# Neighbourhood attention: the keys held as four contiguous column tiles, where one map was read in strided runs

## The reference

```python
def neighbourhood_attention(q, k, v, rpb):        # 8 heads of 64, a grid 64 columns wide
    ...
    c0 = np.clip(cols - WIN_COLS // 2, 0, GRID_W - WIN_COLS)      # window: 8 rows x 16 columns
    ...
        s = jnp.einsum('bqhd,brqchd->bhqrc', q_r, k_win).astype(jnp.float32)
        s = s + bias.transpose(0, 2, 1, 3)[None]
        p = jax.nn.softmax(s.reshape(bsz, H, GRID_W, wr * WIN_COLS), axis=-1)
        return jnp.einsum('bhqrc,brqchd->bqhd', p, v_win)
```

## Time and profile before

| what | value |
|---|---|
| three runs | 3501.95, 3507.84 (median), 3510.64 us |
| the profiled execution | 3500.29 us, its span 3498.5 us |
| mean granted TensorE clock | 0.966 of full speed |
| PE busy | 3202.0 us, 92% |
| DVE busy | 2169.9 us, 62% |
| ACT busy | 1415.3 us, 40% |
| POOL busy | 544.7 us, 16% |

### The profile page before, as it was taken

The page is one execution under the profiler, slowest core; times in us unless marked ns, Lnnn a source line. Parts: engine busy times, 40 slices in busy tenths (PEclk is TensorE's granted clock), DMA queues, the critical chain, the costliest instruction groups (busy, mean ns, idle before and its releaser), DMA issues. The chain is left out here.

```text
span 3498.5 us, 49075 instructions
## 1 busy us (share of the span) xinstructions
PE 3202.0 (92%) x16456; PEld 2663.8 (76%) x16456; DVE 2169.9 (62%) x3352; ACT 1415.3 (40%) x2628; POOL 544.7 (16%) x540
## 2 busy tenths in 40 slices
PE   8999999977999589979939999899998998999999
PEld 6787878765777479967728888678887997888887
DVE  3434536465666589955537666676676997455555
ACT  3343434345766345522223333333333444434443
POOL 2101011012333157735520000000000000000000
PEclk9999999998999899989969999999999999999999
DMA  5354545465331222278852222432233344667776
GB/s 185 127 190 149 193 149 179 136 192 108 85 83 37 68 80 70 65 243 295 275 197 90 102 108 105 144 120 101 97 113 124 134 138 163 215 231 271 244 263 213
DMA packets 394109, 531.94 MB, mean 152 GB/s; under 512 B 126544, under 2 KB 238464, under 8 KB 385328
## 3 DMA queue, kind: packets, MB, share of 16 engines
q1 hardware_dynamic: 378240, 481.97, 42.3%
q0 software_dynamic: 12864, 43.12, 3.4%
q10 hardware_dynamic: 2880, 5.24, 0.4%
HBM read 376.28 MB, written 154.69 MB: 152 GB/s over the span
## 5 line engine op out<-in xcount | busy, mean ns | idle before, releaser
L65 PE MATMUL u_acc<-u_h_hi,u_w_hi 128*128 128x512 f32 (+1 forms) x1848 | 663.2, 359 | 105.9 <-DVE u_h_lo L2316 43.5
L66 PE MATMUL u_acc<-u_h_lo,u_w_hi 128*128 128x512 f32 (+1 forms) x1848 | 660.7, 358 | 0.0
L67 PE MATMUL u_acc<-u_h_hi,u_w_lo 128*128 128x512 f32 (+1 forms) x1848 | 660.2, 357 | 0.0
L65 PEld LDWEIGHTS u_acc<-u_h_hi,u_w_hi 128*128 128x128 f32 x1848 | 353.8, 191 | 162.6 <-issue 69.2
L67 PEld LDWEIGHTS u_acc<-u_h_hi,u_w_lo 128*128 128x128 f32 x1848 | 354.4, 192 | 49.8
L66 PEld LDWEIGHTS u_acc<-u_h_lo,u_w_hi 128*128 128x128 f32 x1848 | 354.4, 192 | 48.6
L454 DVE TENSOR_TENSOR i_w_lo<-i_raw,i_w_hi 128x2048 fp32r<-128x2048 f32 x60 | 140.8, 2347 | 331.7 <-ACT i_w_hi L326 331.7
L2559 ACT CAST d_hi<-d_raw 128x896 fp32r<-128x896 f32 (+1 forms) x231 | 224.2, 979 | 283.8 <-DMA d_raw<-hid_ops 151.2
L2235 ACT CAST u_w_hi<-u_w_sum 128x512 fp32r<-128x512 f32 x264 | 160.4, 620 | 394.0 <-PE u_acc L67 244.5
L2580 DVE TENSOR_TENSOR d_lo<-d_raw,d_hi 128x896 fp32r<-128x896 f32 (+1 forms) x231 | 252.0, 1132 | 106.9 <-ACT d_hi L2559 101.3
L65 PE MATMUL d_acc<-d_hi 128*128 128x512 f32 x770 | 300.9, 391 | 16.1 <-DVE d_lo L2580 11.8
(11 more groups left out here) (250 smaller groups left out, 6286.7 us busy)
## 6 DMA issues: line engine op xcount, KB each, us to landing
u_w_raw<-w_ffn_dram SPq DMA_DIRECT2D x66, 1024.0 KB, 4.9
i_raw<-w_in_dram SPq DMA_DIRECT2D x60, 1024.0 KB, 5.4
d_raw<-wd_ops SPq DMA_DIRECT2D x132, 256.0 KB, 5.2
d_raw<-hid_ops SPq DMA_DIRECT2D x154, 192.0 KB, 6.0
d_raw<-w_down_dram SPq DMA_DIRECT2D x99, 256.0 KB, 5.8
hid_ops<-u_comb SPq DMA_DIRECT2D x88, 256.0 KB, 2.1
d_raw<-hid_ops SPq DMA_DIRECT2D x77, 256.0 KB, 6.6
hid_ops<-u_hid SPq DMA_DIRECT2D x66, 256.0 KB, 2.0
```

Source lines behind the costliest of these rows:

```text
L65: pe.matmul(out, w_hi, x_hi, start=first, stop=False, skip_group_check=resumed)
L66: pe.matmul(out, w_hi, x_lo, start=False, stop=False, skip_group_check=resumed)
L67: return pe.matmul(out, w_lo, x_hi, start=False, stop=last, skip_group_check=resumed)
```

## The change

The keys are held four times over, one tile per column quarter, as `[P, 4, 40, 32]` in place of `[P, 2560]`, so the tiles of a quarter's grid rows are one run of 256, 384 or 512 elements for the score matmuls. An eviction of a band becomes two instructions, each of which writes two quarters (2 x 256 elements) and reads the bank in runs of 32, the quarters' columns overlapping; `ka_out` and `kb_out` count two per band. The masks of the keys are laid out in the same way on the host, so their tensor is 48 x 5120 instead of 48 x 2560; those of the queries keep their form.

```diff
-        ka = [sb(f"ka{i}", [P, T], F32R) for i in range(2)]
-        kb = [sb(f"kb{i}", [P, T], F32R) for i in range(2)]
+        ka = [sb(f"ka{i}", [P, COLT, ROWS, 32], F32R) for i in range(2)]
+        kb = [sb(f"kb{i}", [P, COLT, ROWS, 32], F32R) for i in range(2)]
...
+        def two_tiles(bank, c):
+
+            view = bank.rearrange("p t c -> p (t c)").rearrange("p (r x c) -> p x r c", x=GRID_W // 8, c=8)
+            near = view[:, COL[c] // 8:COL[c] // 8 + 5]
+            return bass.AP(near.tensor, near.offset, [near.ap[0], [8, 2], [GRID_W, 8], [1, 32]])
...
-                    for side, which in ((qb[i], 0), (kb[i], 1)):
-                        pool.dma_start(side[MASK0:MASK0 + MASKS], masks[:, which].bitcast(F32R)) \
-                            .then_inc(masks_set[i], 16)
+                    pool.dma_start(qb[i][MASK0:MASK0 + MASKS], q_masks.bitcast(F32R)).then_inc(masks_set[i], 16)
+                    pool.dma_start(kb[i][MASK0:MASK0 + MASKS], k_masks.bitcast(F32R)).then_inc(masks_set[i], 16)
...
-                dve.tensor_copy(kb[head[1]][0:HEAD, cols], ps_kb[0:HEAD].rearrange("p t c -> p (t c)")) \
-                   .then_inc(kb_out, 1)
+                for c in (0, 2):
+                    dve.tensor_copy(kb[head[1]][0:HEAD, c:c + 2, g * 8:(g + 1) * 8], two_tiles(ps_kb[0:HEAD], c)) \
+                       .then_inc(kb_out, 1)
...
-                act.copy(ka[head[1]][:, cols], ps_ka[:].rearrange("p t c -> p (t c)")).then_inc(ka_out, 1)
+                for c in (0, 2):
+                    act.copy(ka[head[1]][:, c:c + 2, g * 8:(g + 1) * 8], two_tiles(ps_ka[:], c)).then_inc(ka_out, 1)
...
-                wait(pe, ka_out, n)
-                wait(pe, kb_out, n)
+                wait(pe, ka_out, 2 * n)
+                wait(pe, kb_out, 2 * n)
...
                 def keys(x, k):
-                    return x[par][0:k].rearrange("p (r c) -> p r c", c=GRID_W)[:, rows, cols]
-
-                out = ps_s[a % 2][:, 0:COUNT[b] * P].rearrange("p (r c) -> p r c", c=32)
+                    return x[par][0:k, c, rows].rearrange("p r c -> p (r c)")
+
+                out = ps_s[a % 2][:, 0:COUNT[b] * P]
...
-    return m
+    k = m[:, 1].reshape(48, T // GRID_W, GRID_W)
+    return m[:, 0], np.stack([k[:, :, c:c + 32] for c in (0, 8, 24, 32)], axis=1)
```

More of the change, by code:

```diff
@@ L648, in _, with attention_phase @@
             blocks(pe, token_block)
-def attention_phase(nc, q_s, k_s, v_s, copies, masks, ident_dram, mixT):
+def attention_phase(nc, q_s, k_s, v_s, copies, q_masks, k_masks, ident_dram, mixT):
     NT = 20
@@ L884, in out_k_low @@
             def out_k_low(head, g):
-                n, cols = BANDS * number(head) + g, slice(g * TB, (g + 1) * TB)
+                n = BANDS * number(head) + g
                 wait(dve, scored, NT * (number(head) - 1))
                 dve.wait_ge(k_turned, n + 1)
-                dve.tensor_copy(kb[head[1]][0:HEAD, cols], ps_kb[0:HEAD].rearrange("p t c -> p (t c)")) \
-                   .then_inc(kb_out, 1)
+                for c in (0, 2):
+                    dve.tensor_copy(kb[head[1]][0:HEAD, c:c + 2, g * 8:(g + 1) * 8], two_tiles(ps_kb[0:HEAD], c)) \
+                       .then_inc(kb_out, 1)
             def add_bias(head, a):
@@ L1066, in scores @@
                     pe.wait_ge(masks_set[par], 32)
-                    for s in (qa_out, qb_out, ka_out, kb_out):
+                    for s in (qa_out, qb_out):
                         pe.wait_ge(s, BANDS * (number(head) + 1))
+                    for s in (ka_out, kb_out):
+                        pe.wait_ge(s, 2 * BANDS * (number(head) + 1))
                 wait(pe, topped, G - 1)
                 rows = slice(4 * FIRST[b], 4 * (FIRST[b] + COUNT[b]))
-                cols = slice(COL[c], COL[c] + 32)
                 def queries(x, k):
@@ L2643, in build @@
 def build(nc, x, w_in, rpb, w_out, w_ffn, w_down, cols, qk_rows, head_rows, ssm_gain, norm2, ident, ident_bf,
-          tri, tri_masks, masks, y):
+          tri, tri_masks, q_masks, k_masks, y):
     def scratch(name, shape):
@@ L2659, in build @@
     in_proj_phase(nc, x, w_in, cols, qk_rows, rpb, copies, ident, q_s, k_s, v_s, z_s, dtT, xbcT, xcT)
-    attention_phase(nc, q_s, k_s, v_s, copies, masks, ident, mixT)
+    attention_phase(nc, q_s, k_s, v_s, copies, q_masks, k_masks, ident, mixT)
     ssd_phase(nc, xcT, dtT, z_s, head_rows, ssm_gain, tri, tri_masks, ident, ident_bf, mixT)
@@ L2724 @@
     ones, tri_masks = triangles(np)
+    q_masks, k_masks = neighbourhoods(np)
     arrays = dict(
@@ L2731 @@
         ident=np.eye(P, dtype=np.float32), ident_bf=np.eye(P).astype(mybir.dt.np(BF16)),
-        tri=ones, tri_masks=tri_masks, masks=neighbourhoods(np))
+        tri=ones, tri_masks=tri_masks, q_masks=q_masks, k_masks=k_masks)
     arrays = {name + "_dram": np.ascontiguousarray(value) for name, value in arrays.items()}
```

## The result

The changed kernel takes 3529.2 us (median of four runs, 3522.3 to 3533.3) against 3507.3 us before: a ratio of 1.0071 (95% interval 1.0054 to 1.0087), 21.9 us slower where 18.7 were forecast. Its profiled execution took 3527.3 us. From the end of the input projection to the first instruction of the mixer the attention phase took 403.1 us before and 424.8 after, so the phase holds the whole difference of the medians (the two profiled executions lie 27.0 us apart; the 5.3 us outside the phase are of the size by which executions of one kernel differ).

A forecast was written before the change was run, and what follows sets the result against it. Attention's start-up was taken as DMA-bound, its steady part as TensorE's, with ACT's copy closing the ring in half the steps. Masks +6.6, evictions +14.2 and read -2.1 gave +18.7 us, 3526.5 us forecast; 8 in 10 from 3511 to 3540.

The forecast's parts named there:

- The score matmuls: L1080, L1081 on PE: contiguous reads free 4.2 us over 320 matmuls, half under ACT's copy, so -2.1 us.
- the 0.32 us: Time from L1080 to L1081 at 512 columns, put down to the second matmul's weight load, not to the strided read.
- the 13 ns: Most to be gained at a 512-column score matmul from a contiguous read, 0.026 ns a column.
- ACT's casts: High keys' eviction on ACT, doubled: each second cast adds 0.48 us of queue, delaying the copy of the transposed probabilities.
- Step 18: Last eviction step of a head: DVE's second cast delays the finished band's copy, +0.61 us, ACT's hidden under it.
- Head 0's evictions: Head 0's evictions of the next head's five bands, priced like those of other heads at 2.03 us a head.
- The masks: Start of attention: k masks double, 0.98 MB more on POOL's queue with DMA engines full, delaying head 0's values, +6.6 us.
- The absorbed casts: Rival: PE's wait for ACT is only passed on, the four ACT terms go, +8.8, 3516.6 us; chance 0.14.
- the hidden masks: Rival: values wait for something else at the start, so masks cost nothing, +12.1, 3519.9 us; chance 0.09.
- the fast read: Rival: strided read slows score matmuls, 29.8 us less on PE, -9.0 (or +5.9 if half can use it); chance 0.08.
- the slow casts: Rival: casts reading runs take 0.96 us of ACT's queue each, +52.3, 3560.1 us; chance 0.06.

The follow-up runs named there:

- ACT's casts alone: Kernel before, with ACT evicting the high keys twice, the first time into a spare tile: heads 2 to 5 took 46.33 us in the mean.
- DVE's alone: Kernel before, with DVE evicting the low keys twice, the first time into a spare tile: head 4 took 44.74 us against 44.66.
- the second masks late: Changed kernel, with the second parity's mask transfers issued at step 10 of head 0: first weighing at 33.45 us, attention phase 416.0 us against 424.8.
- the masks in rows of 10 KB: Changed kernel, with each k mask transfer cut in two of 48 x 2560 floats: first weighing at 41.85 us, 1.6 earlier.

## Why the prediction was right

- *The score matmuls.* That the read has almost no part in the 0.32 us held. The term was over-sized: -2.1 us forecast, 0.05 us a head measured, 0.4 in all eight. Of the 13 ns that I counted for both matmuls the second gave 11; at the first the pitch moved by 3 ns (321 to 318 at 512 columns, medians of heads 2 to 5).
- *ACT's casts.* 0.48, 0.31, 0.16 and 0.47 us were forecast for the steps 4, 8, 12 and 15; the table gives 0.48, 0.31, 0.15 and 0.48. Reading, for each place, what was already waited for and by how much was enough.
- *Step 18* is the step that failed: +0.61 through DVE was forecast, with ACT's cast hidden under it. The step from 19 to the next head grew by 0.27 us in heads 1, 2 and 4, 0.57 in head 3 and 0.48 in head 5. ACT's casts alone give 0.27 in heads 1 to 4, DVE's alone 0.43 in head 3 and 0.07 in head 4. In the mean of heads 2 to 5 the term is 0.40 us, not 0.61. I had read PE's wait of 0.69 us for DVE, and not PE's next one for ACT; why the heads 3, 5 and 6 pay more (0.47 to 0.57) than the heads 1, 2 and 4 stays open.
- *Head 0's evictions* were priced at 2.0 us like the others. From step 8's scores to head 1's, where they tell, head 0 took 30.65 us before and 32.28 after: they cost 1.6. The table has only 0.4 because the stretch from the first weighing to step 8 was 1.2 us shorter (18.07 for 19.30); with the old evictions it took 18.28 and 17.96 us in two other runs, so nothing shows that the change shortened it.
- *The masks* were 6.6 by the queue's own share of the engines, and 7.9 us in the trace; 6.1 to 6.3 of it are the bytes, the rest came with the rows of 20 KB.
- *Not forecast:* heads 1 and 6 took 2.7 and 3.1 us more, not 1.8. In both PE's granted clock stood at 1.2 GHz at the start: in head 1 for 6.3 us, where the kernel before had 3.4, in head 6 for 3.4, where it had none (below).

The mechanism held; that the sum is so near is in part luck. A steady head was forecast at 1.77 us (2.03 less 0.26 of the read) and measured at 1.82, because step 18 came out 0.21 too dear and the read's gain 0.21 too large. The masks were too cheap by 1.3 us, 2.2 us of clock were left out, and against them stand the 1.2 us that head 0 happened to gain. The absorbed casts, the hidden masks, the fast read and the slow casts are each refuted by a run or by the groups above.

## What to carry to other kernels

A layout that makes a matmul's read contiguous is worth what the pitch of the strided read shows, and here, with runs of 32 columns, that was almost nothing, while the engines that write the layout pay for every copy of it. An added instruction on an engine that is busy for 69% of the stretch (ACT's 200.44 of 291 us in the earlier trace rows) costs its full length where it stands ahead of the one that the busiest engine waits for, and can cost nothing a few instructions earlier, so look for the place before the count. Where two waits of one engine follow each other, lengthening the first costs only what the second does not give back.

## What the runs showed of the hardware

- With the DMA engines full, the first weighing came 1.6 us later when the k masks, 1.97 MB to 48 partitions, went out in two transfers with rows of 20 KB than in four with rows of 10 KB. Their queue's share of the 16 engines from 765 to 860 us was only 0.4 us larger (21.3 for 20.9% of 95 us), so most of the 1.6 is not in the mean time of its packets; where it arises was not shown.
- ACT's copies of 512 elements are recorded with 0.58 us and follow each other at 0.48; the recorded length would overprice a cast by a fifth.
- PE's granted clock fell to the lower level, 1.2 GHz, for 3.4 us at the start of head 6, 2.0 us after PE had stood for 1.4 us waiting for DVE at the end of head 5. It fell there in the runs of the change, of the second masks late, of ACT's cast twice (where PE had stood for 0.82 and 0.55 us) and of DVE's cast twice, not in the one before. In the run with the masks in rows of 10 KB PE stood for the same 1.42 us, and the clock stayed at 2.4 GHz. The stretch in the changed kernel (length, busy us by engine, clock, DMA share, GB/s):

```profile
1089.90:1091.30 1.40, 0.04 (x1) 0.00 (x0) 1.37 (x3) 1.40 (x5) 0.04 (x1) 1.00 0.00 0
1091.30:1093.30 2.00, 1.89 (x11) 1.26 (x12) 1.00 (x7) 1.66 (x6) 0.00 (x0) 1.00 0.13 23
1093.30:1096.70 3.40, 3.40 (x14) 2.31 (x13) 1.75 (x9) 1.77 (x5) 2.03 (x3) 0.50 0.65 151
```

From step 0's to step 2's scores head 6 took 3.9 us there, 2.8 before. Like waits at the ends of the heads 1 to 4 of this run left the clock alone too; why this one did not is open.
